# One decoder step with attention: the two halves of a weight tile split at the ends of different heads

## The chip, the cores and the metric

The kernel is one program on 1 core of one Trainium2 chip. The metric is the device time of one execution in microseconds (us). Three executions of the kernel before took 1636.31, 1636.94 and 1640.3 us; the median is 1636.94 us.

## What is computed

A two-layer decoder for 256 prompt tokens and 8 sample tokens (264 columns in all), width 1024, everything in fp32:

```
layer 0: x += S5 state-space mixer with GLU(rmsnorm(x));  x += dense SwiGLU(rmsnorm(x))
kv     = rmsnorm(x) @ w_kv                     # 4 kv heads of 64
q      = rmsnorm(x) @ w_q                      # 16 heads of 64
s      = q k^T * SCALE + relative bias; window of 128, one learned sink per head
p      = exp(s - m) / (sum exp(s - m) + exp(sink - m)),  m = max(max s, sink)
x     += (p v) @ w_o
x     += top-2-of-8 mixture of SwiGLU experts;  y = rmsnorm(x)
```

Outputs are y, the state of the mixer and the new k/v windows.

## The kernel before, in words

Weights are cut into tiles of 128 x 2048 numbers (1 MB each). Tiles 0 to 50 are those of the dense part (`GLU0`, `GU0`, `DN0`, `KV0` = 41, `Q0` = 43, `O0` = 47, `NDENSE` = 51); behind them come 42 tiles for each of the 8 experts. SyncE loads them into a ring of `RING` = 6 buffers `raw`; a buffer is free for tile n + 6 when tile n is split.

A matrix product is made in three passes of an "fp32r" type (lines 1670 to 1672, `passes`): high x high, low x high and high x low. So each tile has to be split first: ScalarE copies `raw` to `WH` (line 649, the function `hi`), which rounds it to the high part, and VectorE makes `WL` = raw - WH (line 1178, `lo`). Each does a tile in two halves of 128 x 1024. `WH` and `WL` have `SPLIT` = 3 buffers, so tile n may be split when tile n - 3 is used up; the two splits of tile n + 3 are therefore written next to the work that uses tile n.

The order of each engine's work is written out by hand, and engines meet at semaphores only. Each engine works through its own list in order, so a wait stops all that is written behind it.

The attention is a loop over 17 units u = 0 to 16 (`UNITS`; called heads below): u = 0 to 12 and 14 to 16 are the 16 heads of the prompt tokens, and u = 13 is the one unit of the 8 sample tokens. The same loop is written on three engines:

- TensorE, for each u: `score(u)` (q k^T, lines 1763 and 1764, for u = 13 line 1771); for u < 12 `q_quarter`, a quarter of the query product of tiles 44 to 46 (12 matmuls, lines 1670 to 1672; tile 44 in u = 0 to 3, tile 45 in 4 to 7, tile 46 in 8 to 11); then `mix(u - 3)` (p v, lines 1795 to 1797, for the sample unit line 1807) and `turn(u - 2)` (transposes of p, line 1781).
- VectorE, for each u: `scores(u)` (scale, bias and maximum, lines 1254 to 1264), `probs(u - 1)` (1 / sum and the first block of p, lines 1279 to 1282), and for u >= 5 `unit_out(u - 4)` (work at odd heads and the sample unit alone, lines 1297 and 1298).
- ScalarE, for each u: for even u from 2 to 12 first `q_out(u // 2 + 1)` (line 761: the finished query half from PSUM to `QT`), which TensorE needs before its next query half, since both use PSUM bank 7; then `exps(u)` (lines 778 to 783), `second_block(u - 1)` (line 792), `turned_out(u - 2)` (line 800: the transposed p to `PTT`, which `mix` needs).

Into this loop the splits of tiles are put: `hi(dense(Q0 + SPLIT + u // 4))` behind the other work of u = 4, 8 and 12 on ScalarE, and the same `lo` there on VectorE. These are tiles 47, 48 and 49, the first three of the output product. Tile 46, the last of the query product, is split ahead of the loop.

Behind the loop TensorE makes the output product (`o_first` for tile 47, between the last heads, then `pair` for 48 to 50), then come the norm, the router and the experts.

Of the kernel before, what the change touches and what calls it, by code (L numbers as in the profile page):

```python
# [79 lines left out]
def build(nc, xT, xu, gu, vecs, wd, we, wr, a_re, a_im, log_dt, bq, bx, cq, cx, h0q, h0x,  # L80
          kcT, vc, sinks, relb, onehot,
          yT, hp_out, hs_out, kp_out, vp_out, ks_out, vs_out):
    with ExitStack() as ctx:
# [431 lines left out]
        def _(act):  # L515
# [124 lines left out]

            def hi(tile):

                slot_ = tile[2] % RING
                act.wait_ge(loaded[slot_], loads(act, tile))
                if tile[0] is not None or tile[2] >= SPLIT:
                    act.wait_ge(used, at(act, tile, 1 - SPLIT))
                for i in range(2):
                    cols = slice(i * TILE // 2, (i + 1) * TILE // 2)
                    a.copy(WH[tile[2] % SPLIT][:, cols], raw[slot_][:, cols]).then_inc(sem("hi_made"), 1)  # L649
# [102 lines left out]
            for i in range(2):  # L752
                a.copy(QT[:, i, :], ps[:, 2 * (Q0 % 2) + i, 0:NT]).then_inc(sem("q_ready"), 1)
            hi(dense(Q0 + SPLIT))

# [46 lines left out]
            for u in range(NU):  # L802
                if u in (2, 6, 10):
                    q_out(u // 2 + 1)
                if u in (4, 8, 12):
                    q_out(u // 2 + 1)
                if u == 12:
                    new_queries()
                exps(u)
                if u >= 1 and UNITS[u - 1] < NH:  # L810
                    second_block(u - 1)
                if u >= 2:
                    turned_out(u - 2)
                if u in (4, 8, 12):
                    hi(dense(Q0 + SPLIT + u // 4))
                if u == 7:
                    act.wait_ge(sem("k_ready"), 2)
                    act.wait_ge(sem("cache_loaded"), 16 * (TS + 1))
                    a.copy(KCT[:, :, :, W - 1].rearrange("p b k -> p k b"), KT[:, :, TP:NT]).then_inc(sem("kc_ready"), 1)
# [95 lines left out]
        def _(dve):  # L915
# [256 lines left out]

            def lo(tile):

                for i in range(2):
                    cols = slice(i * TILE // 2, (i + 1) * TILE // 2)
# [63 lines left out]
            scale_and_split(XQ, G_MIX1, sem("xq_ready"), 12, XQL, XQH)  # L1240
            for n in range(KV0, Q0 + 1):
                lo(dense(n + SPLIT))
# [58 lines left out]
            for u in range(NU):  # L1301
# [4 lines left out]
                if u >= 5:  # L1306
                    unit_out(u - 4)
                if u in (4, 8, 12):
                    lo(dense(Q0 + SPLIT + u // 4))
            probs(NU - 1)  # L1310
# [758 lines left out]
```

## Time and profile before

| | |
|---|---|
| median of 3 executions | 1636.94 us |
| the profiled execution: its own time | 1638.2 us |
| the profiled execution: span | 1636.4 us |
| TensorE busy | 1510.4 us (92%) |
| VectorE busy | 1252.6 us (77%) |
| ScalarE busy | 996.3 us (61%) |
| mean granted TensorE clock | 0.954 |
| stretch of the experts | about 601 to 1611 us |
| stretch of the loop over heads | about 457.9 to 546.0 us |

The span runs from the first to the last instruction of the profiled execution, and its own time is a little longer. A busy TensorE is not one at its peak. A granted clock of 1.00 is 2.4 GHz, 0.50 is 1.2 GHz. Stretches of time are in us from the start of the span.

### The profile page before, as it was taken

What the parts mean: (1) busy time and instruction counts of PE and PEld (TensorE: products, weight loads), DVE (VectorE), ACT (ScalarE), POOL (GpSimd) and SP (SyncE); (2) the same over time, 40 slices, a digit from 0 to 9 for tenths busy, and PEclk for the clock granted to TensorE, in tenths of its full rate; (3) what the DMA queues carried; (4) which work ended last, traced back from release to release, by engine and by line L of the source; (5) the groups of instructions that cost most, each with busy time, mean ns of one, the idle gap of its engine ahead of it and who ended that gap; (6) DMA issues with size and microseconds to landing.
All of it is one profiled execution on the core that took longest, in us unless ns stands there. A gap on an engine that the chain in (4) does not pass through costs nothing.

```text
span 1636.4 us, 23515 instructions
## 1 busy us (share of the span) xinstructions
PE 1510.4 (92%) x8247; PEld 1287.5 (79%) x8248; DVE 1252.6 (77%) x1522; ACT 996.3 (61%) x1299; POOL 121.1 (7%) x142
## 2 busy tenths in 40 slices
PE   2589989999888879999998999998999999999995
PEld 1578989999776868888887888887888888888884
DVE  7844555554656459999987989987999988999993
ACT  3443444433455337777765777766777777777772
POOL 3971103000100000000000000000000000000000
PEclk9589999999988979999999999999999999999997
DMA  2004579544422219999987999987999988999980
GB/s 101 26 1 162 185 130 314 184 170 180 155 102 110 78 51 362 362 364 354 359 321 295 359 374 353 362 324 292 363 370 352 364 345 325 366 365 353 368 328 28
DMA packets 61947, 423.66 MB, mean 259 GB/s; under 512 B 8302, under 2 KB 8454, under 8 KB 11665
## 3 DMA queue, kind: packets, MB, share of 16 engines
q1 hardware_dynamic: 58784, 412.37, 66.8%
q0 software_dynamic: 3056, 9.85, 3.0%
q8 instruction: 68, 1.11, 0.3%
q14 instruction: 39, 0.32, 0.1%
HBM read 415.31 MB, written 6.88 MB: 258 GB/s over the span
## 4 chain that ended last, share of the span: by engine, by line
PE 89%; DVE 7%; ACT 3%; issue 1%; DMA 0%; SPq 0%; DVEq 0%; ACTq 0%
PE ps L1670 26%; PE ps L1672 25%; PE ps L1671 25%; PE ps L1889 2%; PE ps L1902 1%; PE ps L1558 1%; PE ps L1500 1%; PE ps L1589 1%; PE ps L1915 1%; PE ps L1590 1%; PE ps L1536 1%; DVE WL L1178 1%; ACT TM L613 0%; PE ps L1857 0%; DVE rstd L939 0%
## 5 line engine op out<-in xcount | busy, mean ns | idle before, releaser
L1178 DVE TENSOR_TENSOR WL<-raw,WH 128x1024 fp32r<-128x1024 f32 x774 | 906.1, 1222 | 138.5 <-ACT WH L649 138.2
L649 ACT CAST WH<-raw 128x1024 fp32r<-128x1024 f32 x774 | 772.5, 1049 | 181.1 <-PE ps L1672 181.1
L1670 PE MATMUL ps<-WH,XEH 128*128 128x512 f32 x896 | 362.0, 404 | 10.4 <-issue 8.9
L1672 PE MATMUL ps<-WH,XEL 128*128 128x512 f32 x896 | 353.1, 394 | 0.0
L1671 PE MATMUL ps<-WL,XEH 128*128 128x512 f32 x896 | 351.4, 392 | 0.0
L1670 PEld LDWEIGHTS ps<-WH,XEH 128*128 128x128 f32 x896 | 169.3, 189 | 45.5 <-issue 9.3
L1672 PEld LDWEIGHTS ps<-WH,XEL 128*128 128x128 f32 x896 | 169.3, 189 | 42.8
L1671 PEld LDWEIGHTS ps<-WL,XEH 128*128 128x128 f32 x896 | 169.6, 189 | 35.3
L1670 PE MATMUL ps<-WH,AFH 128*128 128x512 f32 x448 | 178.2, 398 | 0.0
L1671 PE MATMUL ps<-WL,AFH 128*128 128x512 f32 x448 | 176.8, 395 | 0.0
L1672 PE MATMUL ps<-WH,AFL 128*128 128x512 f32 x448 | 176.8, 395 | 0.0
L1670 PE MATMUL ps<-XNH,WH 128*128 128x264 f32 x496 | 145.1, 293 | 9.7 <-DVE XNL L957 9.7
L1671 PE MATMUL ps<-XNL,WH 128*128 128x264 f32 x496 | 143.1, 289 | 0.0
L1672 PE MATMUL ps<-XNH,WL 128*128 128x264 f32 x496 | 143.0, 288 | 0.0
L1670 PEld LDWEIGHTS ps<-XNH,WH 128*128 128x128 f32 x496 | 96.0, 194 | 10.8 <-issue 10.5
L1672 PEld LDWEIGHTS ps<-WH,AFL 128*128 128x128 f32 x448 | 84.3, 188 | 19.9
L1670 PEld LDWEIGHTS ps<-WH,AFH 128*128 128x128 f32 x448 | 84.4, 188 | 18.7
L1671 PEld LDWEIGHTS ps<-WL,AFH 128*128 128x128 f32 x448 | 84.4, 188 | 18.5
L1671 PEld LDWEIGHTS ps<-XNL,WH 128*128 128x128 f32 x496 | 96.2, 194 | 0.2
L1672 PEld LDWEIGHTS ps<-XNH,WL 128*128 128x128 f32 x496 | 95.7, 193 | 0.0
L857 ACT CAST AFH<-ps 128x512 fp32r<-128x512 f32 x56 | 33.0, 589 | 66.7 <-PE ps L1902 66.7
L708 ACT ACTIVATE SG<-ps 128x264 f32<-128x264 f32 x30 | 11.8, 392 | 90.8 <-PE ps L1672 90.8
(358 smaller groups left out, 1783.7 us busy)
## 6 DMA issues: line engine op xcount, KB each, us to landing
raw<-in_we SPq DMA_DIRECT2D x336, 1024.0 KB, 5.2
raw<-in_wd SPq DMA_DIRECT2D x51, 1024.0 KB, 4.9
bias_rows<-SC POOLq DMA_DIRECT2D x1, 3072.0 KB, 37.1
BIAS<-bias_rows POOLq DMA_DIRECT2D x16, 128.0 KB, 9.3
U<-in_xu SPq DMA_DIRECT2D x1, 1280.0 KB, 7.2
X<-in_xT SPq DMA_DIRECT2D x1, 1056.0 KB, 9.6
out_yT<-XN SPq DMA_DIRECT2D x2, 528.0 KB, 2.7
out_ks<-KCT POOLq DMA_DIRECT2D x1, 1024.0 KB, 5.1
```

The costliest lines, as they stand in the source:

```text
L649: a.copy(WH[tile[2] % SPLIT][:, cols], raw[slot_][:, cols]).then_inc(sem("hi_made"), 1)
L857: a.copy(AFH[:, 4 * j:4 * j + 4, :], ps[:, 6 + j % 2, :].rearrange("p (c n) -> p c n", c=4))\
L1178: v.tensor_tensor(WL[tile[2] % SPLIT][:, cols], raw[tile[2] % RING][:, cols], WH[tile[2] % SPLIT][:, cols].bitcast(F32), ALU.subtract).the ...
L1500: t_.matmul(ps[:, NORM_BANK[i], 0:NT], ones[:, :], SQ[:, c % 2, :], start=(c == 0), stop=(c == KC - 1))\
L1536: mm = t_.matmul(ps[:, 6 + b % 2, g * UC:(g + 1) * UC], AT[:, 4 * (b % 2) + g, :], U[:, hf * GH + 4 * b + g, :], start=True, stop=True)
L1558: mm = t_.matmul(ps[:, 2 + b % 2, g * P:(g + 1) * P], AM[:, hf * GH + 4 * b + g, :], CM[hf][:, 4 * b + g, :], start=True, stop=True)
L1589: t_.matmul(out, U[:, 4 * u + g, :], TM[hf][:, k, :], start=True, stop=False)
L1590: mm = t_.matmul(out, HM[:, k, :], CM[hf][:, k, :], start=False, stop=True)
L1670: t_.matmul(out, sh, mh, start=first, stop=False)
L1671: t_.matmul(out, sh, ml, start=False, stop=False)
L1672: return t_.matmul(out, sl, mh, start=False, stop=last)
L1889: mm = t_.matmul(ps[:, i, c * 2 * P:(c + 1) * 2 * P], part[:, t, (2 * i + c) * P:(2 * i + c + 1) * P], DSP[:, t, :], start=(t == 0 and par ...
```

## The change

The two halves of a tile's split no longer stand together. On ScalarE the high halves of a tile are now at the ends of two heads that follow one another (u = 1 and 2, 5 and 6, 9 and 10, 13 and 14), and on VectorE the low halves at the ends of u = 2 and 3, 6 and 7, 10 and 11, 14 and 15: each low half one head behind its high half. Tile 46 is now one of the four that are split inside the loop (in u = 1 to 3); its split ahead of the loop is gone on both engines.

```diff
-            def hi(tile):
+            def hi(tile, halves=(0, 1)):
 
                 slot_ = tile[2] % RING
-                act.wait_ge(loaded[slot_], loads(act, tile))
-                if tile[0] is not None or tile[2] >= SPLIT:
-                    act.wait_ge(used, at(act, tile, 1 - SPLIT))
-                for i in range(2):
+                if halves[0] == 0:
+                    act.wait_ge(loaded[slot_], loads(act, tile))
+                    if tile[0] is not None or tile[2] >= SPLIT:
+                        act.wait_ge(used, at(act, tile, 1 - SPLIT))
+                for i in halves:
...
-            hi(dense(Q0 + SPLIT))
...
-                if u in (4, 8, 12):
-                    hi(dense(Q0 + SPLIT + u // 4))
+                if u < NU - 2 and u % 4 in (1, 2):
+                    hi(dense(Q0 + SPLIT + u // 4), (u % 4 - 1,))
...
-            def lo(tile):
-
-                for i in range(2):
+            def lo(tile, halves=(0, 1)):
+
+                for i in halves:
...
-            for n in range(KV0, Q0 + 1):
+            for n in range(KV0, Q0):
                 lo(dense(n + SPLIT))
...
-                if u in (4, 8, 12):
-                    lo(dense(Q0 + SPLIT + u // 4))
+                if 1 < u < NU - 1 and u % 4 in (2, 3):
+                    lo(dense(Q0 + SPLIT + u // 4), (u % 4 - 2,))
```

TensorE's list is the same in both kernels. Two places of the other lists follow; in these rows L649 of the kernel before is L650 of the changed one, L753 is L754.

ScalarE, the entry to the loop and heads 0 to 2, before:

```order
L753 COPY QT<-ps 128x264 x2
L649 CAST WH<-raw 128x1024 x2
L778 ACT_TABLE_LOAD
L778 ACTIVATE SC,sm<-SC,nm 128x128
L781 ACTIVATE SC,sm<-SC,nm 128x256
L783 ACTIVATE es<-nm,SINK 128x2
L778 ACTIVATE SC,sm<-SC,nm 128x128
L781 ACTIVATE SC,sm<-SC,nm 128x256
L783 ACTIVATE es<-nm,SINK 128x2
L792 ACTIVATE SC<-SC,rd 128x256
L761 COPY QT<-ps 128x264
```

and in the changed kernel:

```order
L754 COPY QT<-ps 128x264 x2
L778 ACT_TABLE_LOAD
L778 ACTIVATE SC,sm<-SC,nm 128x128
L781 ACTIVATE SC,sm<-SC,nm 128x256
L783 ACTIVATE es<-nm,SINK 128x2
L778 ACTIVATE SC,sm<-SC,nm 128x128
L781 ACTIVATE SC,sm<-SC,nm 128x256
L783 ACTIVATE es<-nm,SINK 128x2
L792 ACTIVATE SC<-SC,rd 128x256
L650 CAST WH<-raw 128x1024
L761 COPY QT<-ps 128x264
```

Both halves of tile 46 went from in front of the loop; the first of them now stands between `second_block` of head 0 and the copy of the query half (L761) with which head 2 begins. The same pattern (a half directly in front of L761) comes again at the ends of heads 5 and 9.

ScalarE, heads 12 and 13 (the sample unit), before:

```order
L771 COPY SG<-QT 64x4x4 x8
L778 ACTIVATE SC,sm<-SC,nm 128x128
L781 ACTIVATE SC,sm<-SC,nm 128x256
L783 ACTIVATE es<-nm,SINK 128x2
L792 ACTIVATE SC<-SC,rd 128x256
L800 COPY PTT<-ps 128x384
L649 CAST WH<-raw 128x1024 x2
L778 ACTIVATE SC,sm<-SC,nm 128x128
L786 ACTIVATE es<-nm,SINKC 128x1
L792 ACTIVATE SC<-SC,rd 128x256
L800 COPY PTT<-ps 128x384
L778 ACTIVATE SC,sm<-SC,nm 128x128
```

and in the changed kernel:

```order
L771 COPY SG<-QT 64x4x4 x8
L778 ACTIVATE SC,sm<-SC,nm 128x128
L781 ACTIVATE SC,sm<-SC,nm 128x256
L783 ACTIVATE es<-nm,SINK 128x2
L792 ACTIVATE SC<-SC,rd 128x256
L800 COPY PTT<-ps 128x384
L778 ACTIVATE SC,sm<-SC,nm 128x128
L786 ACTIVATE es<-nm,SINKC 128x1
L792 ACTIVATE SC<-SC,rd 128x256
L800 COPY PTT<-ps 128x384
L650 CAST WH<-raw 128x1024
L778 ACTIVATE SC,sm<-SC,nm 128x128
```

The pair of halves of tile 49 went from between heads 12 and 13; its first half is now behind head 13, its second behind head 14.

VectorE, heads 6 to 8 of the changed kernel (`probs` of head 5 in the first three rows):

```order
L1279 TENSOR_TENSOR rd<-sm,es 128x2
L1280 RECIPROCAL rd<-rd 128x2
L1282 TENSOR_SCALAR SC<-SC,rd 128x128
L1178 TENSOR_TENSOR WL<-raw,WH 128x1024
L1254 SCALAR_TENSOR_TENSOR SC<-ps,BIAS 128x128
L1257 SCALAR_TENSOR_TENSOR SC<-ps,BIAS 128x256
L1261 TENSOR_REDUCE mx<-SC 128x1
L1263 TENSOR_REDUCE mx<-SC 128x1
L1264 TENSOR_SCALAR nm<-mx,SINK 128x2
```

Before, no L1178 stands there: both low halves of tile 47 stood together between heads 4 and 5. Now one is behind head 6 and one behind head 7.

## Rows read from the trace of the kernel before

**Rows 1.** Windows: us, busy of PE, PEld, DVE, ACT, POOL, PEclk, DMA, GB/s
```profile
457.90:546.00 88.10, 75.20 (x491) 59.57 (x491) 47.59 (x158) 46.13 (x143) 2.37 (x4) 0.85 0.23 86
601.00:1611.00 1010.00, 997.25 (x4540) 816.08 (x4538) 898.59 (x861) 739.65 (x817) 0.00 (x0) 0.99 0.90 340
```
**Rows 2.** Timeline of PE: where it stood in the loop (start, us, idle before)
```profile
466.44 0.39 PE L1670 MATMUL ps<-XQH,WH 128*128 128x264 f32 x1 [2.63 <-ACT QT L761]
...
476.28 0.36 PE L1670 MATMUL ps<-XQH,WH 128*128 128x264 f32 x1
...
486.84 0.39 PE L1670 MATMUL ps<-XQH,WH 128*128 128x264 f32 x1 [2.95 <-ACT QT L761]
...
496.25 0.36 PE L1670 MATMUL ps<-XQH,WH 128*128 128x264 f32 x1 [0.26 <-ACT QT L761]
...
506.82 0.39 PE L1670 MATMUL ps<-XQH,WH 128*128 128x264 f32 x1 [2.95 <-ACT QT L761]
...
514.39 0.43 PE L1795 MATMUL ps<-PTT,VT 128*64 128x128 f32 x2
...
518.25 0.43 PE L1795 MATMUL ps<-PTT,VT 128*64 128x128 f32 x2
...
523.64 0.69 PE L1795 MATMUL ps<-PTT,VT 128*64 128x128 f32 x2 [3.20 <-ACT PTT L800]
...
536.05 0.66 PE L1795 MATMUL ps<-PTT,VT 128*64 128x128 f32 x2 [0.66 <-ACT PTT L800]
```
**Rows 3.** Timeline of ACT, end of head 4 and head 5
```profile
479.65 2.00 ACT L649 CAST WH<-raw 128x1024 fp32r<-128x1024 f32 x2
484.58 0.40 ACT L778 ACTIVATE SC<-SC,nm 128x128 f32<-128x128 f32 x1 [2.92 <-DVE nm L1264]
...
485.65 0.49 ACT L792 ACTIVATE SC<-SC,rd 128x256 f32<-128x256 f32 x1
486.05 0.46 ACT L800 COPY PTT<-ps 128x384 f32<-128x384 f32 x1
486.41 0.37 ACT L761 COPY QT<-ps 128x264 f32<-128x264 f32 x1
```
**Rows 4.** Timeline of DVE, the pair of low halves and head 5
```profile
480.74 2.36 DVE L1178 TENSOR_TENSOR WL<-raw,WH 128x1024 fp32r<-128x1024 f32 x2 [2.40 <-ACT WH L649]
483.02 0.28 DVE L1254 SCALAR_TENSOR_TENSOR SC<-ps,BIAS 128x128 f32<-128x128 f32 x1
...
484.84 0.29 DVE L1282 TENSOR_SCALAR SC<-SC,rd 128x128 f32<-128x128 f32 x1
485.05 0.42 DVE L1297 CAST OTH<-ps 128x256 fp32r<-128x256 f32 x1
```
**Rows 5.** Timeline of ACT: two table loads, each with what follows
```profile
457.93 2.00 ACT L649 CAST WH<-raw 128x1024 fp32r<-128x1024 f32 x2
459.95 1.28 ACT L778 ACT_TABLE_LOAD   x1
463.12 0.40 ACT L778 ACTIVATE SC<-SC,nm 128x128 f32<-128x128 f32 x1 [1.88 <-DVE nm L1264]
...
584.54 1.28 ACT L839 ACT_TABLE_LOAD   x1
585.84 0.22 ACT L839 ACTIVATE r<-r 128x24 f32<-128x24 f32 x1
```
**Rows 6.** Windows of PE alone: us, PE busy (x), PEclk, DMA share, GB/s
```profile
467.60:474.40 6.80, 6.80 (x28) 0.50 0.01 2
474.40:488.00 13.60, 10.55 (x70) 1.00 0.21 77
488.00:491.40 3.40, 3.40 (x15) 0.51 0.00 0
491.40:522.20 30.80, 25.69 (x183) 1.00 0.30 113
522.20:539.20 17.00, 14.90 (x105) 0.50 0.16 63
```

## The prediction

> **What bounds the kernel now.** I read the windows first. The loop over heads lasts 88.1 us; TensorE is busy in 75.2 of them at a mean granted clock of 0.85, VectorE in 47.6 and ScalarE in 46.1 [rows 1]. So neither of the two engines that the change touches is full, but TensorE has 12.9 us of gaps, and it lost more to its clock. The expert stretch is 1010 us with TensorE busy in 997 [rows 1]: it starts when the router behind the loop is done and is held by TensorE itself, so what the loop gains or loses should arrive at the end nearly whole. 0.3% of the time, about what a measurement can tell from no change, is 4.9 us.
>
> The timeline of TensorE gives the gaps [rows 2]. Four are large: 2.63 us before the query quarter of head 2 (466.44), 2.95 before that of head 6 (486.84), 2.95 before that of head 10 (506.82) and 3.20 before the mix with which head 14 begins (523.64). That is 11.7 of the 12.9 us. Each lies behind a split. The middle case shows how: ScalarE starts tile 47 at 479.65, both halves take 2.00 us [rows 3]; VectorE has been idle for 2.40 us in front of its low halves and does them from 480.74 for 2.36 us, and only then starts the scores of head 5, at 483.02 [rows 4], though TensorE had made them when it began head 5's work near 480.1 (two heads of its own work after 476.28, less one quarter, mix and turn). The delay goes on through ScalarE's exponentials (484.58) to its query copy L761 (486.41), and TensorE's quarter starts 0.43 us after that [rows 2, 3].
>
> **The cycle of one head.** TensorE's own work per head is (486.84 - 2.95 - 476.28) / 2 = 3.80 us at 2.4 GHz [rows 2]. The chain that must close within it, for every even head, is: scores start to exponentials start 484.58 - 483.02 = 1.56; exponentials 1.07; second block 0.40; turned copy 0.36; query copy to quarter 0.43; with 0.04 to pick the scores up, 3.86 us [rows 2 to 4]. So an even head waits 0.06 even without any split; head 8 waits 0.26 [rows 2], with one more small copy in ScalarE's way. A high half costs 2.00 / 2 = 1.0 us of ScalarE, a low half 2.36 / 2 = 1.2 us of VectorE [rows 3, 4].
>
> **Heads 6 and 10.** The pair and its wait leave. But a high half now stands directly in front of the query copy of heads 6 and 10, in this chain: 3.86 + 1.0 - 3.80 = 1.06 us of wait in place of 2.95, a gain of 1.9 each, **3.8 us**. The second high half stands behind head 6 (10), where ScalarE next waits for the scores of head 7; 3.8 us per head against 1.9 of work and the 1.0 leaves room, so nothing. VectorE needs 485.05 - 483.02 = 2.0 per head for scores and probabilities, 0.8 more at odd heads for `unit_out`, and 1.2 for a half: 3.2 in head 6 fits, 4.0 in heads 7 and 11 is 0.2 too long. That delays the scores of heads 8 and 12, whose results TensorE needs two heads later: nothing.
>
> **Head 2.** Tile 46 leaves the entry. TensorE stands from 463.8 to 466.44 [rows 2]; score(1) was done a quarter and a score earlier, near 461.3, but the scores of head 0 were held to that same time by the low halves of tile 46. Freed, head 1's scores start at 461.35, and the chain without the turned copy but with the new high half (3.86 - 0.04 - 0.36 + 1.0 = 4.46) gives a quarter at 465.8: **0.7 us**. ScalarE's table load has to be done by then. It takes 1.28 us [rows 5]; before, it stood behind the two halves, now it starts near 458.0 and is done at 459.3, ahead of head 0's exponentials (about 460.4). The Trainium skill (ScalarE: Activation LUTs, What ACT_TABLE_LOAD costs) counts about 1.38 us of drain on top, 2.66 in all for a switch; by it the exponentials would start 0.3 us later. The trace differs: 1.30 us after the start of the load at 584.54 the next activation runs [rows 5], so I take no drain.
>
> **Heads 12 to 14.** Between the mix that begins at 514.39 (head 12) and the one at 523.64 lie 9.25 us [rows 2]. The pair of tile 49 is gone from there. TensorE itself would be ready again 6.0 us after 514.39 (mix and turn, the sample scores, at 518.25 the mix and turn of head 13, and one score, together 2.2). The chain: sample scores done at +3.8, on VectorE 0.9 (this unit has no second block), 0.6, 0.4 and 0.5 on ScalarE: +6.2. So the 3.20 us of wait shrink to 0.2, a gain of **3.0 us**.
>
> **The last heads.** The halves of tile 49 now sit at heads 13 and 14 (high) and 14 and 15 (low), in a stretch of 523.64 to 536.05 = 12.4 us [rows 2] where TensorE was at 1.2 GHz [rows 6] and had no query work left. VectorE becomes the chain there: scores and probabilities 2.0, low half 1.2, the same with `unit_out` 4.0, then scores 1.6, exponentials to turned copy 1.9 and a pick-up make 10.8; TensorE's turn of the sample unit's successor ends a little later at 1.2 GHz, some 11.2. I take 1.2 us of gain here. The bounds: if both low halves add to the old 12.4, -2.4; if the clock holds at 2.4 GHz, +2.5.
>
> **The clock.** It was 0.50 for 6.8 us from 467.6 and for 3.4 us from 488.0, in both cases right after a gap, and 0.50 for 17 us from 522.2 [rows 6]; after the equal gap before 506.82 it stayed at 1.00. At half rate, heads 6 to 8 took 496.25 - 486.84 = 9.4 us instead of 2 x 3.80 + 0.26 = 7.9: 1.5 us. With a gap of 1.06 us, well under 2.63, I expect that fall not to come: **1.5 us**. Heads 2 to 4 took 476.28 - 466.44 = 9.8; at full rate it would be 6.9 (two heads of which head 2 has no mix), 2.9 us less. Their gap is still 2.0 us; the nearest measured gap is the 2.63 that brought a fall, so I take 0 of it and keep 2.9 as the bound. For the last heads I take no change of clock.
>
> **Others.** The splits of tiles 46 to 49 end up to two heads later, and with them the loads of the tiles six further on; those are expert tiles, wanted at 601 [rows 1], so some tens of us are left. Tile 46 is wanted at head 8, tile 47 behind the loop: both are ready 4 heads or more ahead. TensorE's list is unchanged, the number of splits too.
>
> **Sum.** 0.7 + 3.8 + 3.0 + 1.2 + 1.5 = 10.2 us. Against the profiled execution's own 1638.2 this is 1628.0, against the median, 1.3 lower, 1626.7. The falls of the clock differ from execution to execution, so I do not carry the difference whole: **1627 us**.
>
> **Rivals.**
> (1) The clock also holds after head 2, since its gap shrinks from 2.63 to 2.0 and 2.95 us were once borne without a fall [rows 2, 6]. Another 2.9 us: 1624. Chance 0.30.
> (2) The clock falls after every gap that remains. Then the 1.5 is not won, and head 10 pays 3.4 us at half rate, 1.7: 10.2 - 1.5 - 1.7 = 7.0, 1630. For it: it fell after three of four large gaps. Against it: nothing fell after 0.26 or 0.66 [rows 2], but there is no gap near 1.06 to read from. The Trainium skill (TensorE: Matmul & The Clock Gate, HAM oscillation) describes a kernel in which a recurring wait between bursts brings the lower rate back each time; by that rule this would be the case. Chance 0.15.
> (3) The gain stays within 4.9 us: the low halves at heads 14 and 15 cost the full 2.4 (-3.6 against my sum) and no clock is won (-1.5): 5.1, and any further wait of a high half takes it under the bound, 1633. A change that does not take the waits away at all would look the same, 1637. Chance 0.10.
> (4) Slower: the clock. Once TensorE falls to 1.2 GHz after head 2's gap it may stay there, because the new shorter gaps come at the same heads while the work between them is slow. 3.4 us at half rate did the work of 1.9, so a head of 3.80 takes 6.8 us, and ten heads (2 to 11) lose 30 us instead of the 4.4 of now; less the 8.7 won in waits that is +17, 1654. It decides at head 4: if the clock is still 0.50 at the quarter of head 6, this is the case. Against it: with the same work it came back after 6.8 and after 3.4 us [rows 6]. Chance 0.03.
>
> **How the numbers follow.** The forecast has 0.42, rival 1 0.30, rival 2 0.15, rival 3 0.10, rival 4 0.03. The forecast, rivals 1 and 2 are gains of more than 4.9 us: 0.87. No change within 4.9: 0.10. Slower: 0.03. Low end: 10.2 + 2.9 and the upper bound of the last heads (+1.3) is 14.4, from 1636.9 about 1622.5, with the spread of the runs below 1622. High end: 1636.9 less the 5.1 of rival 3 is 1631.8, 1632. Outside remain rivals 3 in part and 4.
>
> **What would show it.** Right: gaps of about 2.0, 1.1 and 1.1 us before the quarters of heads 2, 6 and 10, the releaser still L761, and 0.2 before the mix of head 14; two heads between quarters in 7.6 to 8.7 us; VectorE no longer idle for 2.4 us before a low half; the loop in 76 to 79 us. Wrong: gaps of 2.5 us or more at heads 6 or 10, a releaser on VectorE's line 1178, a clock of 0.50 between heads 4 and 11, or a loop shortened with the experts ending no earlier.

## The result, and the profile after

| | before | changed |
|---|---|---|
| executions | 6 | 6 |
| median | 1637.28 us | 1625.93 us |
| lowest to highest | 1636.31 to 1640.3 | 1624.59 to 1627.08 |
| profiled execution: own time, span | 1638.2, 1636.4 | 1626.27, 1624.5 |
| TensorE busy | 1510.4 us | 1505.5 us |
| VectorE, ScalarE busy | 1252.6, 996.3 | 1253.0, 995.7 |

The ratio is 0.9925, with a 95% interval of 0.9914 to 0.9936: 11.35 us less, where 10.2 were forecast; the time lies 1.1 us under the forecast and inside the range. VectorE and ScalarE do the same work as before to within 0.6 us. What changed is when.

The windows of the changed kernel, the loop over heads and then the experts (columns as in [rows 1]):

```profile
457.90:534.50 76.60, 68.33 (x491) 54.63 (x491) 47.93 (x160) 45.88 (x143) 2.36 (x4) 0.93 0.27 99
588.00:1598.00 1010.00, 999.07 (x4549) 817.71 (x4547) 897.91 (x862) 739.07 (x817) 0.00 (x0) 0.99 0.89 340
```

The loop takes 76.6 us where it took 88.1 [rows 1]. TensorE's time without work in it went from 12.9 to 8.3 us, and its busy time from 75.2 to 68.3, with the same 491 matmuls in the records and a mean clock of 0.93 in place of 0.85: the larger part of the gain shows as a faster clock, not as shorter waits. The two stretches of 1010 us were chosen equally long, so they do not show how long the experts take. The first matmul of the experts does, before and then changed:

```profile
602.96 0.51 PE L1670 MATMUL ps<-WH,XEH 128*128 128x512 f32 x1 [1.52 <-DVE XEL L1403]
```

```profile
591.01 0.50 PE L1670 MATMUL ps<-WH,XEH 128*128 128x512 f32 x1 [1.53 <-DVE XEL L1403]
```

It comes 11.95 us earlier, and TensorE's last wait for VectorE's line 1411, at the end of the experts, ends at 1614.68 before and at 1602.77 changed, 11.91 us earlier. The experts take as long as before, and the lead of the loop arrives nearly whole.

The timeline of TensorE in the changed kernel, the instructions that answer to [rows 2]:

```profile
465.86 0.53 PE L1670 MATMUL ps<-XQH,WH 128*128 128x264 f32 x1 [1.93 <-ACT QT L761]
474.25 0.36 PE L1670 MATMUL ps<-XQH,WH 128*128 128x264 f32 x1 [0.18 <-ACT QT L761]
482.87 0.39 PE L1670 MATMUL ps<-XQH,WH 128*128 128x264 f32 x1 [1.02 <-ACT QT L761]
490.78 0.36 PE L1670 MATMUL ps<-XQH,WH 128*128 128x264 f32 x1 [0.27 <-ACT QT L761]
499.40 0.39 PE L1670 MATMUL ps<-XQH,WH 128*128 128x264 f32 x1 [1.02 <-ACT QT L761]
...
506.95 0.43 PE L1795 MATMUL ps<-PTT,VT 128*64 128x128 f32 x2
...
513.31 0.43 PE L1795 MATMUL ps<-PTT,VT 128*64 128x128 f32 x2 [0.30 <-ACT PTT L800]
...
523.86 0.66 PE L1795 MATMUL ps<-PTT,VT 128*64 128x128 f32 x2 [0.66 <-ACT PTT L800]
```

Set against the same instructions before, these give the lead that the changed kernel has won by each point:

| point | before | changed | lead | won in the stretch | forecast |
|---|---|---|---|---|---|
| first score | 457.91 | 458.04 | -0.13 | | |
| quarter of head 2 | 466.44 | 465.86 | 0.58 | 0.7 | 0.7 |
| quarter of head 4 | 476.28 | 474.25 | 2.03 | 1.45 | 0 (up to 2.9) |
| quarter of head 6 | 486.84 | 482.87 | 3.97 | 1.94 | 1.9 |
| quarter of head 8 | 496.25 | 490.78 | 5.47 | 1.50 | 1.5 |
| quarter of head 10 | 506.82 | 499.40 | 7.42 | 1.95 | 1.9 |
| mix in head 12 | 514.39 | 506.95 | 7.44 | 0.0 | 0 |
| mix in head 14 | 523.64 | 513.31 | 10.33 | 2.89 | 3.0 |
| first mix behind the loop | 536.05 | 523.86 | 12.19 | 1.86 | 1.2 |
| last instruction (span) | 1636.4 | 1624.5 | 11.9 | -0.3 | 0 |

The small gaps before the quarters are where they were worked out to be: 1.93, 1.02 and 1.02 us, with line 761 as the releaser. Why they are not zero shows in ScalarE's timeline, end of head 5 and start of head 6:

```profile
481.50 1.04 ACT L650 CAST WH<-raw 128x1024 fp32r<-128x1024 f32 x1
482.45 0.37 ACT L761 COPY QT<-ps 128x264 f32<-128x264 f32 x1
```

The high half stands directly in front of the query copy, and TensorE's quarter starts 0.42 us behind that copy's start. VectorE's timeline, heads 6 to 8:

```profile
481.89 0.29 DVE L1254 SCALAR_TENSOR_TENSOR SC<-ps,BIAS 128x128 f32<-128x128 f32 x1 [0.88 <-PE ps L1764]
...
483.92 1.22 DVE L1178 TENSOR_TENSOR WL<-raw,WH 128x1024 fp32r<-128x1024 f32 x1
...
486.75 0.29 DVE L1254 SCALAR_TENSOR_TENSOR SC<-ps,BIAS 128x128 f32<-128x128 f32 x1 [1.61 <-PE ps L1764]
...
489.58 1.22 DVE L1178 TENSOR_TENSOR WL<-raw,WH 128x1024 fp32r<-128x1024 f32 x1
490.71 0.28 DVE L1254 SCALAR_TENSOR_TENSOR SC<-ps,BIAS 128x128 f32<-128x128 f32 x1
```

No low half has an idle time before it, where the pair waited for 2.40 us [rows 4]: its high half was made a head ago. Behind the low half of head 6 VectorE idles 1.61 us again, and behind that of head 7 it goes on at once, so the odd head is just full.

The clock of the changed kernel in three stretches of the loop (TensorE alone: us, busy, granted clock, DMA share, GB/s):

```profile
465.90:469.30 3.40, 3.40 (x15) 0.51 0.02 5
469.40:520.20 50.80, 45.78 (x330) 1.00 0.30 110
520.20:527.20 7.00, 6.34 (x68) 0.53 0.43 152
```

It was at half rate for 3.4 and just under 7 us, against 6.8, 3.4 and 17 before [rows 6].

### The profile page after: what moved, and what is told of

It reads as the page before. It is cut to its first block, busy times and chain, and to the rows that moved or that the text cites. A ratio compares the mean times of both kernels' runs of the same rounds, so it can differ in the third digit from the quotient of the medians.

```text
span 1624.5 us, 23515 instructions
## 1 busy us (share of the span) xinstructions
PE 1505.5 (93%) x8247; PEld 1283.9 (79%) x8248; DVE 1253.0 (77%) x1522; ACT 995.7 (61%) x1299; POOL 120.5 (7%) x142
## 4 chain that ended last, share of the span: by engine, by line
PE 89%; DVE 7%; ACT 3%; issue 1%; DMA 0%; SPq 0%; DVEq 0%; ACTq 0%
PE ps L1670 26%; PE ps L1672 25%; PE ps L1671 25%; PE ps L1889 2%; PE ps L1902 2%; PE ps L1500 1%; PE ps L1558 1%; PE ps L1589 1%; PE ps L1915 1%; PE ps L1590 1%; PE ps L1536 1%; ACT TM L613 1%; PE ps L1857 0%; DVE rstd L939 0%; DVE AM L1065 0%
## 5 line engine op out<-in xcount | busy, mean ns | idle before, releaser
L1178 DVE TENSOR_TENSOR WL<-raw,WH 128x1024 fp32r<-128x1024 f32 x774 | 906.4, 1222 | 126.9 <-ACT WH L650 126.4
L650 ACT CAST WH<-raw 128x1024 fp32r<-128x1024 f32 x774 | 772.9, 1049 | 181.2 <-PE ps L1672 181.1
L1670 PE MATMUL ps<-WH,XEH 128*128 128x512 f32 x896 | 362.3, 404 | 9.7 <-issue 8.2
L1670 PEld LDWEIGHTS ps<-WH,XEH 128*128 128x128 f32 x896 | 169.5, 189 | 44.8 <-issue 8.6
L1670 PE MATMUL ps<-WH,AFH 128*128 128x512 f32 x448 | 178.1, 398 | 0.0
L1670 PE MATMUL ps<-XNH,WH 128*128 128x264 f32 x496 | 144.3, 291 | 9.9 <-DVE XNL L957 9.9
L1670 PEld LDWEIGHTS ps<-XNH,WH 128*128 128x128 f32 x496 | 95.0, 192 | 11.2 <-issue 10.5
L1670 PEld LDWEIGHTS ps<-WH,AFH 128*128 128x128 f32 x448 | 84.4, 188 | 18.6
```

The lines of the kernel that those rows point to most:

```text
L1178: v.tensor_tensor(WL[tile[2] % SPLIT][:, cols], raw[tile[2] % RING][:, cols], WH[tile[2] % SPLIT][:, cols].bitcast(F32), ALU.subtract).the ...
L1670: t_.matmul(out, sh, mh, start=first, stop=False)
```

## The experiments

Runs made together share a chip and a figure for the kernel before on it (1639.5, 1638.44 or 1639.7 us); the ratio to that figure is what can be compared between runs that were not made together. "Gap" is TensorE's idle time in the profiled execution.

### What each of two properties is worth: the halving and the lag

Two runs take one property of the change away each. The first keeps the low halves a head behind the high ones but does both halves together:

```diff
-                if u < NU - 2 and u % 4 in (1, 2):
-                    hi(dense(Q0 + SPLIT + u // 4), (u % 4 - 1,))
+                if u < NU - 2 and u % 4 == 1:
+                    hi(dense(Q0 + SPLIT + u // 4))
...
-                if 1 < u < NU - 1 and u % 4 in (2, 3):
-                    lo(dense(Q0 + SPLIT + u // 4), (u % 4 - 2,))
+                if u < NU - 1 and u % 4 == 2:
+                    lo(dense(Q0 + SPLIT + u // 4))
```

> The changed kernel without the halving: both high halves of a tile at the end of heads 1, 5, 9 and 13, both low halves one head later (2, 6, 10, 14). Theory (a high half in front of the query copy is on the chain in full, a low half is free as long as VectorE's head fits in 3.80 us): 2.0 us of high halves in the chain give gaps of 3.86 + 2.0 - 3.80 = 2.1 us before the quarters of heads 6 and 10 and 2.9 before head 2's; two low halves make VectorE's even head 2.0 + 2.4 = 4.4 us, 0.6 too long, which adds 0.3 to 0.6 to head 8. Per tile 1.0 to 1.6 us more than the changed kernel, 3.5 to 5 us in all, and the clock falls after at least one gap more: 1629.5 to 1633. Rival (the lag of one head, by which VectorE no longer waits for ScalarE, is the whole gain, and the halving does nothing): 1626, gaps of 1.0 us.

Measured: 1634.42 us against 1639.5 for the kernel before, ratio 0.9971 (0.9961 to 0.9980): by the ratio 4.8 us faster than before, and 7 to 10 us slower than the changed kernel (0.9925 and, in a run below, 0.9910). The rival falls, but the cost is larger than the 3.5 to 5 us expected. Its timeline of TensorE, the gaps of the loop:

```profile
466.75 0.59 PE L1670 MATMUL ps<-XQH,WH 128*128 128x264 f32 x1 [2.87 <-ACT QT L761]
...
487.33 0.39 PE L1670 MATMUL ps<-XQH,WH 128*128 128x264 f32 x1 [1.98 <-ACT QT L761]
495.23 0.36 PE L1670 MATMUL ps<-XQH,WH 128*128 128x264 f32 x1 [0.29 <-ACT QT L761]
504.80 0.39 PE L1670 MATMUL ps<-XQH,WH 128*128 128x264 f32 x1 [1.97 <-ACT QT L761]
```

The gaps of 2.87, 1.98 and 1.97 us are those of the theory (2.9, 2.1, 2.1): each is 0.95 us more than in the changed kernel, the one high half that was added in front of the query copy. The other part of the theory failed: the low pair, 0.6 us too long for a head, did not add to head 8, whose gap stayed at 0.29. The late query copy had pushed TensorE's next scores back too, and VectorE even idled for 1.44 us before them. Two parts of the larger cost show in the profile. Behind the gap of 2.87 the clock was at 0.50 for 10.2 us (465.9 to 476.1), so that heads 2 to 6 took 20.58 us in place of 17.01 in the changed kernel's first profile. And the pair of tile 49 in the last heads made the gaps there 1.13 and 2.08 us in place of 0.71 and 1.37, with a clock at 0.50 for 10.3 us: 12.47 us from the mix in head 14 to the first mix behind the loop, in place of 10.55.

The second keeps the halves apart but puts each low half at the end of the same head as its high half:

```diff
-                if 1 < u < NU - 1 and u % 4 in (2, 3):
-                    lo(dense(Q0 + SPLIT + u // 4), (u % 4 - 2,))
+                if u < NU - 2 and u % 4 in (1, 2):
+                    lo(dense(Q0 + SPLIT + u // 4), (u % 4 - 1,))
```

> The changed kernel without the lag: the halves stand apart, but each low half at the end of the same head as its high half (1 and 2, 5 and 6, 9 and 10, 13 and 14). Theory: VectorE comes to the low half 2.0 us after it has taken up the scores of a head and the high half is done after 1.56 + 1.07 + 0.40 + 0.36 + 1.0 = 4.4 us, so it idles 2.4 us and takes up the next scores at 5.6 in place of 3.8: 1.8 us late. The head after that is late too. The gap before head 6 stays 1.0 (its copy does not hang on these scores), but the mix and the quarters of heads 7 and 8 wait some 2 to 3 us in all: per tile about 2.5 us more than the changed kernel, with head 2 and the last heads 8 to 10 us in all: 1634 to 1636. Rival (the halving is the whole gain): 1626 to 1627.

Measured: 1642.67 us, ratio 1.0026 (1.0015 to 1.0036), so by the ratio slower than the kernel before by 4.3 us. The direction of the theory holds and the rival (1626 to 1627) falls, but the cost is larger than the 8 to 10 us over the changed kernel that I gave it: by the ratios 16 us and more. VectorE's timeline, heads 6 and 7:

```profile
486.76 1.23 DVE L1178 TENSOR_TENSOR WL<-raw,WH 128x1024 fp32r<-128x1024 f32 x1 [1.57 <-ACT WH L650]
487.90 0.28 DVE L1254 SCALAR_TENSOR_TENSOR SC<-ps,BIAS 128x128 f32<-128x128 f32 x1
...
492.37 1.23 DVE L1178 TENSOR_TENSOR WL<-raw,WH 128x1024 fp32r<-128x1024 f32 x1 [2.36 <-ACT WH L650]
493.51 0.28 DVE L1254 SCALAR_TENSOR_TENSOR SC<-ps,BIAS 128x128 f32<-128x128 f32 x1
```

VectorE stands still in front of both halves, 1.57 and 2.36 us, and the scores wait behind it. The timeline of TensorE shows what that makes:

```profile
476.90 0.36 PE L1670 MATMUL ps<-XQH,WH 128*128 128x264 f32 x1 [2.15 <-ACT QT L761]
487.05 0.39 PE L1670 MATMUL ps<-XQH,WH 128*128 128x264 f32 x1 [1.04 <-ACT QT L761]
497.53 0.49 PE L1670 MATMUL ps<-XQH,WH 128*128 128x264 f32 x1 [2.86 <-ACT QT L761]
507.68 0.39 PE L1670 MATMUL ps<-XQH,WH 128*128 128x264 f32 x1 [1.03 <-ACT QT L761]
517.69 0.43 PE L1795 MATMUL ps<-PTT,VT 128*64 128x128 f32 x2 [2.39 <-ACT PTT L800]
```

Heads 2, 6 and 10 have the gaps of the changed kernel, and heads 4, 8 and 12 have new ones of 2.15, 2.86 and 2.39 us. In the last heads come two more, of 3.02 and 2.75 us, where the changed kernel has 0.71 and 1.37. From the first score to the first mix behind the loop it takes 82.36 us in place of 65.82; about 10.6 of the 16.5 us are these longer gaps. The rest, some 6 us, goes with the clock: it was at 0.50 behind each gap of 1.9 us or more, four times for 3.4 us and at the end for 13.7. The expectation had the gaps about right and left out the clock. Halving without the lag makes two stalls per tile out of one. So neither property gives the whole gain by itself, and they are not equal: the lag takes VectorE's wait away, and the halving then keeps what is left short enough to fit.

### What each tile is worth

Tile 46 alone moved into the loop, tiles 47 to 49 as before (in this and the next run `hi` and `lo` take halves as in the change; that part of the edit is not shown):

```diff
-            hi(dense(Q0 + SPLIT))
...
+                if u in (1, 2):
+                    hi(dense(Q0 + SPLIT), (u - 1,))
                 if u in (4, 8, 12):
                     hi(dense(Q0 + SPLIT + u // 4))
...
-            for n in range(KV0, Q0 + 1):
+            for n in range(KV0, Q0):
...
+                if u in (2, 3):
+                    lo(dense(Q0 + SPLIT), (u - 2,))
                 if u in (4, 8, 12):
                     lo(dense(Q0 + SPLIT + u // 4))
```

> The kernel before with one part of the change alone: tile 46 is split inside the loop (high halves at the ends of heads 1 and 2, low halves at 2 and 3), tiles 47 to 49 stay pairs at heads 4, 8 and 12. Theory (each gap is worth what its wait shrinks by): the gap before head 2's quarter is 1.9 us in place of 2.63, the gaps before heads 6 and 10 stay at 2.9 and that before head 14 at 3.2. The gain is 0.6 us of wait and, where the clock falls for 3.4 us in place of 6.8 after head 2, another 1.5: 2.1 us below the kernel before, 1635.2. Rival (taking a split out of the entry is what pays, since all later heads start earlier with a warm clock): 5 us or more, under 1632.

Measured: 1638.28 against 1639.5 us, ratio 0.9991 (0.9982 to 1.0): 1.5 us by the ratio, with an interval that reaches down to nothing. The gaps in its timeline are 1.92, 2.96, 2.96 and 3.21 us, as expected; the rival falls.

Tiles 47 and 48 alone as in the change, tile 46 at the entry and tile 49 as a pair at head 12:

```diff
-                if u in (4, 8, 12):
-                    hi(dense(Q0 + SPLIT + u // 4))
+                if 4 < u < 12 and u % 4 in (1, 2):
+                    hi(dense(Q0 + SPLIT + u // 4), (u % 4 - 1,))
+                if u == 12:
+                    hi(dense(O0 + 2))
...
-                if u in (4, 8, 12):
-                    lo(dense(Q0 + SPLIT + u // 4))
+                if 4 < u < 12 and u % 4 in (2, 3):
+                    lo(dense(Q0 + SPLIT + u // 4), (u % 4 - 2,))
+                if u == 12:
+                    lo(dense(O0 + 2))
```

> The kernel before with the change made for tiles 47 and 48 alone (high halves at heads 5, 6, 9 and 10, low halves at 6, 7, 10 and 11); tile 46 is split at the entry and tile 49 as a pair at head 12, as before. Theory (the parts add up): gaps of 1.0 us before the quarters of heads 6 and 10 in place of 2.95, 3.9 us, and of the clock's falls behind those gaps, one or two in each execution of the kernel before at 1.5 each, none: 5.4 to 6.9 us below the kernel before, with gaps of 2.6 and 3.2 left at heads 2 and 14. Rival (a gap only moves: what is won at heads 6 and 10 is lost at the next wait): under 3 us.

Measured: 1633.39 against 1639.7 us, ratio 0.9964 (0.9952 to 0.9976), 5.9 us by the ratio. The gaps are 2.63, 1.02, 1.02 and 3.36. No fall of the clock came between heads 4 and 13. The rival falls.

The changed kernel with tile 49 alone put back:

```diff
-                if u < NU - 2 and u % 4 in (1, 2):
+                if u < 12 and u % 4 in (1, 2):
                     hi(dense(Q0 + SPLIT + u // 4), (u % 4 - 1,))
+                if u == 12:
+                    hi(dense(O0 + 2))
...
-                if 1 < u < NU - 1 and u % 4 in (2, 3):
+                if 1 < u < 12 and u % 4 in (2, 3):
                     lo(dense(Q0 + SPLIT + u // 4), (u % 4 - 2,))
+                if u == 12:
+                    lo(dense(O0 + 2))
```

> The changed kernel with tile 49 alone put back as a pair at the end of head 12, on both engines. Theory (the pair's wait in front of the sample unit's scores is worth 3.0 us, and the halves at heads 13 to 15 cost less than they displace): the gap before head 14's mix is 3.2 us again, the clock falls behind it for the rest of the loop, and the stretch from that mix to the first mix behind the loop is 12.4 us in place of 10.6: 3.0 + 1.8 = 4.8 us above the changed kernel. Rival (the last heads hide either placing, since they are bound by VectorE in any case): 0 to 2 us above.

The changed kernel itself ran beside it:

> The changed kernel itself, on the chip of the runs beside it. Both theories: 11 to 12 us below the kernel before; gaps of 1.9, 1.0 and 1.0 us before the quarters of heads 2, 6 and 10. It shows how far the clock's falls in the loop differ from execution to execution: a fall after head 2's gap of 1.9 us may come or not.

Measured: 1632.13 us with tile 49 put back and 1624.88 for the changed kernel, the kernel before 1638.44; ratios 0.9957 (0.9944 to 0.9971) and 0.9910 (0.9895 to 0.9926). Tile 49 is worth 7.2 us by the medians and 7.7 by the ratios, more than the 4.8 expected; the rival (0 to 2) falls. In the timeline with tile 49 put back, the mix of head 14, the first mix behind the loop and the start of the output product behind the last mix are (L1799 and L1674 are there what L1795 and L1670 are in the changed kernel)

```profile
516.81 0.43 PE L1799 MATMUL ps<-PTT,VT 128*64 128x128 f32 x2 [3.35 <-ACT PTT L800]
...
528.51 0.66 PE L1799 MATMUL ps<-PTT,VT 128*64 128x128 f32 x2 [0.66 <-ACT PTT L800]
540.77 0.39 PE L1674 MATMUL ps<-OTH,WH 128*128 128x264 f32 x1 [0.98 <-DVE OTL L1300]
```

and the same three in the changed kernel beside it:

```profile
512.71 0.43 PE L1795 MATMUL ps<-PTT,VT 128*64 128x128 f32 x2 [0.30 <-ACT PTT L800]
...
523.39 0.66 PE L1795 MATMUL ps<-PTT,VT 128*64 128x128 f32 x2 [0.66 <-ACT PTT L800]
534.35 0.39 PE L1670 MATMUL ps<-OTH,WH 128*128 128x264 f32 x1 [0.98 <-DVE OTL L1298]
```

The gap of 3.35 us is back in place of 0.30: the 3.0 of the theory. From the mix of head 14 to the first mix behind the loop 11.70 us in place of 10.68, and from there to the output product 12.26 in place of 10.96. The last figure is the part that the expectation had left out. With tile 49 put back, the clock was at half rate from 517.7 to 534.8, beyond the loop; in the changed kernel from 519.8 to 526.6. The three differences are 3.05, 1.02 and 1.30, together 5.4 us. The two profiled executions differ by 1.5 us more in the loop, at heads 2 to 4, where the clock fell behind equal gaps of 1.93 and 1.92 us in one and not in the other; that part has nothing to do with tile 49. What fills 5.4 up to the 7.2 of the medians stays open.

Do the parts add up? Tile 49's part is itself a difference to the changed kernel, so the test is the other two: tile 46 alone and tiles 47 and 48 alone give 1.5 + 5.9 = 7.4 us by the ratios, and the kernel with all three moved and tile 49 put back gives 7.0 (0.9957). Within their intervals (1.5 to 2.2 us to either side) they add up, and nothing shows that a gap is merely moved on.

### Whether the rest is the high half in front of the query copy

In the changed kernel the first high half of tile 46 moved from head 1 to head 0:

```diff
-                if u < NU - 2 and u % 4 in (1, 2):
+                if u == 0:
+                    hi(dense(Q0 + SPLIT), (0,))
+                if 1 < u < NU - 2 and u % 4 in (1, 2):
                     hi(dense(Q0 + SPLIT + u // 4), (u % 4 - 1,))
```

> The changed kernel with one move: the first high half of tile 46 at the end of head 0 in place of head 1, where it stood in front of head 2's query copy. Theory: the gap before head 2's quarter falls from 1.9 to 1.0 us, and with a gap that short the clock does not fall there: 0.9 + 1.5 = 2.4 us below the changed kernel. Rival (the clock falls there whatever the gap, because the first two heads have no mix and no turns): 0.9 us below.

Measured: 1625.61 us, ratio 0.9923 (0.9909 to 0.9936), beside 1624.88 and 0.9910 for the changed kernel. In the time, neither the 2.4 us nor the rival's 0.9 shows. In the profiled executions the mechanism is there: the gap before head 2's quarter is 0.98 in place of 1.92 us, and the mix of head 14 comes 508.44 - 455.61 = 52.83 us after the first score, in place of 512.71 - 458.92 = 53.79. In these two executions two things stand against the gain. First, the clock did not fall behind the gap of 1.92 us in that execution of the changed kernel either: its heads 2 to 4 took 473.60 - 466.74 = 6.86 us, at full rate, where they took 8.39 in the first one. Second, the fall in the last heads lasted longer here. The clock in the two executions, this run first, then the changed kernel beside it (TensorE alone, columns as in [rows 6]):

```profile
455.60:514.80 59.20, 53.16 (x362) 1.00 0.30 110
514.90:525.90 11.00, 10.34 (x97) 0.54 0.27 97
```

```profile
458.90:519.80 60.90, 53.94 (x386) 1.00 0.29 107
519.90:526.60 6.70, 6.04 (x56) 0.50 0.46 159
```

Some 10 us at the low rate (the window of 11.0 has a mean of 0.54) in place of 6.7, and the 1 us lead of head 14 is gone at the output product (75.99 us after the first score against 75.43). That is one execution of each, so how often a longer fall comes stays open; this pair shows that a longer fall of the clock can take back a shorter gap. It does not show where the medians' difference comes from, since the profiled execution of this run was the faster of the two (1623.02 against 1625.43 us).

All high halves at even heads, where no query copy stands behind them, and the low halves at even heads too:

```diff
-                if u < NU - 2 and u % 4 in (1, 2):
-                    hi(dense(Q0 + SPLIT + u // 4), (u % 4 - 1,))
+                if u < NU - 2 and u % 2 == 0:
+                    hi(dense(Q0 + SPLIT + u // 4), (u % 4 // 2,))
...
-                if 1 < u < NU - 1 and u % 4 in (2, 3):
-                    lo(dense(Q0 + SPLIT + u // 4), (u % 4 - 2,))
+                if u >= 2 and u % 2 == 0:
+                    lo(dense(Q0 + SPLIT + (u - 2) // 4), ((u - 2) % 4 // 2,))
```

> Another placing: high halves at the ends of the even heads 0, 2, ... 14, none in front of the query copy of an even head, and each low half two heads later, at the even heads 2, 4, ... 16, where VectorE has no work of unit_out. Theory (the remaining gaps of the changed kernel are the high half in front of the query copy): gaps of 1.0 before head 2's quarter in place of 1.93 and 0.1 before those of 6 and 10 in place of 1.02, that is 0.9 + 0.9 + 0.9 = 2.7 us, and with a gap of 1.0 before head 2 the clock does not fall there, 1.5 more: 1621.7 us. In the last heads a low half at 14 and at 16 in place of 14 and 15 is worth 0 to 1. Rival (the gaps come from the chain through the scores, not from the high half's place): the same 1625.9.

Measured: 1622.7 us beside 1639.5, ratio 0.9901 (0.9886 to 0.9917). By the time alone this is not clear of the changed kernel: its interval reaches 0.9917, and theirs begin at 0.9914 and 0.9895. The idle times of TensorE in its timeline from 470 to 530:

```profile
472.75 0.36 PE L1670 MATMUL ps<-XQH,WH 128*128 128x264 f32 x1 [0.15 <-ACT QT L761]
488.35 0.36 PE L1670 MATMUL ps<-XQH,WH 128*128 128x264 f32 x1 [0.28 <-ACT QT L761]
509.95 0.43 PE L1795 MATMUL ps<-PTT,VT 128*64 128x128 f32 x2 [0.30 <-ACT PTT L800]
512.86 0.43 PE L1795 MATMUL ps<-PTT,VT 128*64 128x128 f32 x2 [0.71 <-ACT PTT L800]
516.21 2.04 PE L1807 MATMUL ps<-PTT,VC 128*64 128x4 f32 x64 [1.37 <-ACT PTT L800]
519.53 0.66 PE L1795 MATMUL ps<-PTT,VT 128*64 128x128 f32 x2 [0.66 <-ACT PTT L800]
```

The gaps before the quarters of heads 6 and 10 are gone from the list, and that before head 2 is 0.98. They were the high half in front of the query copy, as the theory says, not the chain through the scores: the low halves moved too in this run, but the kernel with the lag alone, where each such gap grew by the 0.95 us of one more high half, points the same way.

The same placing, with tile 49 out of the loop:

```diff
-                if u < NU - 2 and u % 2 == 0:
+                if u < 12 and u % 2 == 0:
                     hi(dense(Q0 + SPLIT + u // 4), (u % 4 // 2,))
             second_block(NU - 1)
             turned_out(NU - 2)
+            hi(dense(O0 + 2))
             turned_out(NU - 1)
...
-                if u >= 2 and u % 2 == 0:
+                if 2 <= u < 14 and u % 2 == 0:
                     lo(dense(Q0 + SPLIT + (u - 2) // 4), ((u - 2) % 4 // 2,))
             probs(NU - 1)
-            for u in range(NU - 4, NU):
+            for u in range(NU - 4, NU - 1):
                 unit_out(u)
+            lo(dense(O0 + 2))
+            unit_out(NU - 1)
```

> The placing at even heads for tiles 46 to 48, and tile 49 out of the loop: its high pair between ScalarE's last two turned copies, its low pair in VectorE's wait of 7.7 us ahead of the last unit_out. Theory: as the even placing (3 to 4 us below the changed kernel), and without a half in the last heads the scores of heads 15 and 16 are taken up 0.8 and 1.9 us earlier, which shortens the gap of 1.4 us before the sample unit's mix by 0.8 and what follows by up to 1 more: 4 to 6 us below the changed kernel, 1620 to 1622. Rival (TensorE's own chain of turn, copy and mix bounds the last heads): the same as the even placing, 1622.7.

Measured: 1621.43 us beside 1638.44, ratio 0.9894 (0.9878 to 0.9910). That is inside the 1620 to 1622 expected, but only 3.5 us under the changed kernel beside it (1624.88) where 4 to 6 were forecast. Since the even placing had run in another group, beside other executions of the kernel before, both ran once more beside each other:

> The placing at even heads a second time, beside the next run on the same chip. Theory: 3 us below the changed kernel, 1621.5 to 1623; no fall of the clock before head 14. Rival (what the short gaps win is given back by an earlier fall of the clock in the last heads, as where only head 0 was used): 0 to 1 us below the changed kernel.

> The placing at even heads with tile 49 behind the loop, a second time, to tell it from the even placing on one chip. Theory: the gap before the sample unit's mix is 0.7 in place of 1.4 us, and the loop 0.7 us shorter than with the even placing: 0.5 to 1 us below it. Rival (VectorE's scores of heads 15 and 16 matter in full): 2 us or more below it.

Measured: 1623.76 us (ratio 0.9908, 0.9893 to 0.9923) and 1619.78 us (ratio 0.9882, 0.9867 to 0.9897), the kernel before 1639.7. The first lies outside its 1621.5 to 1623; its ratio is 0.3 to 2.8 us below the changed kernel's two, so the time does not decide between its theory and its rival. The second is 4 us faster than the first by the medians, where its theory had 0.5 to 1 and its rival 2 or more, and its interval just meets the other's. In its timeline (where L1810 and L1798 stand for L1807 and L1795) the gap before the sample unit's mix is half of what it was, as expected:

```profile
512.17 2.04 PE L1810 MATMUL ps<-PTT,VC 128*64 128x4 f32 x64 [0.68 <-ACT PTT L800]
515.34 0.66 PE L1798 MATMUL ps<-PTT,VT 128*64 128x128 f32 x2 [0.66 <-ACT PTT L800]
```

and its clock was low for under 4 us in all of the loop (us, busy, granted clock):

```profile
455.60:514.90 59.30, 55.57 (x425) 1.00 0.30 110
515.00:518.70 3.70, 3.36 (x16) 0.54 0.00 0
```

In that execution the clock fell after the sample unit's mix and not in it: its 64 small matmuls, as in the even placing's first execution, took 2.04 us, where they took 3.58 before and 2.80 in the changed kernel. From the first score to the output product it took 526.20 - 455.66 = 70.54 us, the even placing beside it 531.98 - 457.93 = 74.05. Of these 3.5 us the wait is 0.7, as the theory has it; the even placing's clock was low for 10.3 us in that stretch, some 6.6 more, which is about the other 3 us at half rate. The first profiles of the two placings, on one chip but in different groups, are a cleaner pair, since the clock was low in them for nearly the same time (6.9 and 6.8 us): 531.59 - 459.02 = 72.57 us with tile 49 in the loop and 529.70 - 457.83 = 71.87 with it behind, 0.7 apart, the wait alone. So the wait's 0.7 us is shown; whether tile 49's place also brings longer time at full rate, or the medians' 4 us are in part luck, is not settled by four profiles. Against the changed kernel's second profile, both profiles of the even placing were 2.9 us shorter from the first score to the mix in head 14 (50.93 and 50.89 us against 53.79). From there to the output product the first took the same 21.64 us, and the second 23.16, which gave 1.5 of them back. The even placing with tile 49 behind the loop is the fastest version of the study, 17 to 20 us under the kernel before by the medians.

## Why the prediction was right

**The cycle and its chain.** The chain of 3.86 us against TensorE's 3.80 per head was the centre of the argument. It gave 1.06 us for heads 6 and 10 (measured 1.02 and 1.02) and, without the turned copy, 2.0 for head 2 (1.93); the chain worked out for the sample unit gave 0.2 for head 14 (0.30). The runs confirm it from both sides: a whole high pair in its place gives 1.98 and 1.97, and no half gives no gap there.

**Each term.** Head 2: 0.7 forecast and measured (the working itself, 466.44 less 465.8, gives 0.6). Heads 6 and 10: 3.8 forecast, 3.9 measured. Heads 12 to 14: 3.0 and 2.9, and 3.05 when tile 49 was put back. Heads 6 to 8, the clock: 1.5 and 1.50; this is the difference to the one profiled execution of the kernel before, in which the clock fell there. ScalarE's table load, taken at its 1.28 us with no drain behind it, fits: the load began at 458.19, and the first exponentials ran at 460.63, after 1.16 us of waiting for their shift from VectorE.

**The cost that was taken as nothing** held: the second high halves, the low halves at heads 7 and 11, and the later loads of the expert tiles. Between the first matmul of the experts and the end of TensorE's last wait for line 1411 lie 1011.76 us, where it was 1011.72.

**The two terms that were off.** The clock behind head 2 was put at 0 with 2.9 as the bound. It gave 1.45, since the clock fell for 3.4 us and not 6.8, and in the second profiled execution of the changed kernel it did not fall at all: the full 2.9. So rival 1 is not another case but a matter of the execution, and the value taken, by the nearest gap, was too careful. The last heads were put at 1.2 with no change of clock; they gave 1.86, because the clock stayed high up to 520.2, through the mixes in heads 14 and 15 and the first part of the sample unit's mix. My sum for that stretch of 12.4 us was bounded by TensorE at 1.2 GHz, 11.2 us; it took 10.55. It has two parts. Up to the sample unit's mix it took 6.26 us, with waits for line 800 (7.33 before), and the same 6.26 or 6.27 in the four other profiles with a wait of 1.37 us there. From that mix on it took 4.29 us, against 5.08 before, and this part goes with the clock: 4.97 with the half at head 0, where the clock was at half rate for nearly all of it, and 3.32 in the even placing's first profile, where the 64 small matmuls ran at full rate. So the 1.2 is about what comes out when the clock falls early (1.18 with the half at head 0), and the rest is the clock. Both errors have one sign: in both places I kept the clock's fall as it was in the kernel before, though the gap in front of it was to shrink from 2.63 to 2.0 and from 3.20 to 0.2 us.

**What was luck.** How close the time came. The terms were worked out against one profiled execution of the kernel before, with falls of the clock that differ from execution to execution; the lead in the profiles is 11.9 us, that of the medians 11.35, and when it ran again the changed kernel was 13.6 us under the kernel before.

**The rivals.** Rival 2, a fall behind every remaining gap, did not come: nothing fell behind 1.02 us, in any of the runs. The kernel in the Trainium skill's account of a recurring wait (TensorE: Matmul & The Clock Gate, HAM oscillation) waits for some 3 to 5 us each time; I had applied it to gaps of 1 us, and there the traces do not bear it out. Behind the gaps of 2.96 and 3.21 us in the kernel with tile 46 alone moved, the clock did fall every time. Its price for a fall of 3.4 us, 1.7, was also a little high against the 1.5 of heads 6 to 8. Rival 3 named the low halves of heads 14 and 15 as a cost. They do cost something: in the even placing, without the halves of tile 49 in the last heads, the gap before the sample unit's mix is 0.7 us shorter, but not 2.4. Rival 4 would have needed a clock at 0.50 at the quarter of head 6, and it was at 1.00.

**What was not tried.** The head loop was never run at a forced half rate, so the 6.8 us per head of rival 4 is not measured. Whether the clock falls behind a gap was read from one profile of each run, so a chance of it can be counted over the runs but was not measured for one kernel.

## What to carry to other kernels

When two engines hand a piece of side work to each other inside a loop, the piece costs the second engine's wait as well as its own time; writing the second part one turn later takes that wait away, and only then does cutting the piece smaller help. Cutting alone made two stalls of one here, and a slower kernel. Then look what stands directly behind each piece in the engine's list: the same 1.0 us was free behind an even head and a full 1.0 us of TensorE's time in front of the copy that it waits for.

## What the runs showed of the hardware

Behind equal gaps TensorE's clock did not do the same in each execution: in the kernel before, after a gap of 2.95 us it fell for 3.4 us once and stayed at full rate once [rows 2, 6]. Over the profiles of the loop, 15 gaps of 2.15 to 3.36 us began at full rate, and in 14 of them or behind them the clock fell. After a gap of 1.92 or 1.93 us before head 2's quarter it fell in four of five profiles; the one without a fall is the changed kernel's second, and its first is one of the four. After the gaps of 1.98 and 1.97 us in the kernel with the lag alone it did not fall. After gaps of 0.97 to 1.04 us in front of query work it was never low. In the last heads, which have no query work, it fell in every profile, even where no gap there was above 0.71 us (tile 49 behind the loop), and came back only after the output product had begun. From the mix in head 14 to the output product behind the last mix, the changed kernel took 21.64 us with the clock low for 6.8, and the kernel with the half at head 0 took 23.16 with 10.2: what a change wins in front of such a stretch can be lost in it again, here 1.5 us.

The stretches outside the loop are not equal to the last us either: the first score came between 455.61 and 459.02 us in these profiles, though nothing written ahead of the entry differs. A part of 1 us can therefore be read from a gap in the trace, and hardly from the time.
